# Another order of the maxima and their transposes in the attention of a four-layer backbone

## The reference, cut to what matters

```python
s = einsum('bqhgd,bkhd->bhgqk', q, k) * scale      # latent queries: 512 cached + 1024 latent keys
p = softmax(s, axis=-1)                            # windowed layer: 512 cached + keys within 128, and a sink
o = einsum('bhgqk,bkhd->bqhgd', p, v)              # context queries: 256 context keys
```

## Time and profile before

| what | value |
|---|---|
| three runs, median (lowest to highest) | 3683.17 us (3682.59 to 3685.68) |
| the profiled execution | 3670.98 us, its span 3669.2 us |
| mean granted clock of PE | 0.987 |
| PE busy | 3471.0 us, 95% of the span |
| DVE busy | 2547.2 us, 69% |
| ACT busy | 2166.3 us, 59% |
| POOL busy | 904.4 us, 25% |
| attention of layers 0, 1, 2, 3 | from 399.8, 1337.7, 2207.7, 3026.2 us of the span |

### The profile page before, as it was taken

One profiled execution on the slowest core, in us unless ns is written; L12 is line 12 of the kernel. 1 busy time (PEld: TensorE's weight loads), 2 busy tenths in 40 slices (PEclk: granted clock), 3 DMA queues, 4 the chain that ended last, 5 costly groups with the idle time before them and its releaser, 6 DMA issues. The chain is left out here.

```text
span 3669.2 us, 80042 instructions
## 1 busy us (share of the span) xinstructions
PE 3471.0 (95%) x33644; PEld 2061.8 (56%) x33644; DVE 2547.2 (69%) x3728; ACT 2166.3 (59%) x2859; POOL 904.4 (25%) x739
## 2 busy tenths in 40 slices
PE   6999999999999989999999998888999989999998
PEld 3554566666455555565555565666455545666654
DVE  6426788888457559999755518989553458888864
ACT  5424677877434348888733217777334338888861
POOL 0000144343220014444411001222220003444432
PEclk8999999999999999999999999999999999999999
DMA  6127533332112342333111425443112382222211
GB/s 255 48 85 224 146 80 75 71 83 62 72 36 70 118 127 65 81 78 76 28 72 61 118 95 134 100 97 71 68 43 71 120 225 64 55 55 57 49 54 58
DMA packets 373318, 325.35 MB, mean 89 GB/s; under 512 B 246272, under 2 KB 294080, under 8 KB 371424
## 3 DMA queue, kind: packets, MB, share of 16 engines
q1 hardware_dynamic: 372960, 320.24, 32.1%
HBM read 228.94 MB, written 91.23 MB: 87 GB/s over the span
## 5 line engine op out<-in xcount | busy, mean ns | idle before, releaser
L2242 PE MATMUL bank<-q_slots,k_slots 96*128 96x512 f16 (+7 forms) x3968 | 1050.0, 366 | 26.2 <-PEq L1436 16.2
L798 PE MATMUL bank<-H_hilo,w_hilo 128*128 128x512 f16 (+1 forms) x5760 | 1044.8, 344 | 11.8 <-DVE w_hilo L1048 8.3
L2061 DVE TENSOR_REDUCE max_parts<-bank 128x1 f32<-128x512 f32 (+2 forms) x1536 | 954.0, 644 | 115.4 <-PE bank L2005 110.2
L2318 ACT ACTIVATE p_f<-bank 128x1024 f32<-128x1024 f32 (+2 forms) x768 | 743.0, 967 | 316.6 <-PE bank L2242 300.1
L798 PEld LDWEIGHTS bank<-H_hilo,w_hilo 128*128 128x128 f16 x5760 | 563.4, 98 | 493.0 <-DVE w_hilo L1048 9.3
L2366 DVE TENSOR_TENSOR p_lo<-p_f,p_hi 128x1024 f16<-128x1024 f32 (+2 forms) x576 | 712.7, 1237 | 63.3 <-ACT p_hi L2325 60.1
L2325 ACT ACTIVATE p_hi<-bank 128x1024 f16<-128x1024 f32 (+2 forms) x768 | 740.3, 964 | 0.0
L2005 PE MATMUL bank<-k_slots,q_slots 96*128 96x512 f16 (+4 forms) x1536 | 565.6, 370 | 42.5 <-DVE max_parts L2061 36.5
L2429 POOL TENSOR_TENSOR p_lo<-p_f,p_hi 128x1024 f16<-128x1024 f32 x192 | 414.3, 2158 | 549.8 <-ACT p_hi L2325 549.8
L2242 PEld LDWEIGHTS bank<-q_slots,k_slots 96*128 96x128 f16 (+2 forms) x3968 | 345.7, 98 | 285.2 <-issue 51.3
L1012 ACT ACTIVATE z_ring<-bank 128x512 f32<-128x512 f32 (+1 forms) x192 | 87.5, 528 | 428.6 <-PE bank L798 414.0
(11 more groups left out here) (205 smaller groups left out, 4054.9 us busy)
## 6 DMA issues: line engine op xcount, KB each, us to landing
ada_w<-in_w_ada SPq DMA_DIRECT2D x48, 768.0 KB, 6.3
gate<-z_ring SPq DMA_DIRECT2D x32, 640.0 KB, 3.3
gate_rows<-gate SPq DMA_DIRECT2D x32, 640.0 KB, 3.9
q_slots<-q_mla SPq DMA_DIRECT2D x64, 240.0 KB, 3.2
k_mla<-H_hilo SPq DMA_DIRECT2D x64, 224.0 KB, 3.2
k_slots<-k_mla SPq DMA_DIRECT2D x64, 224.0 KB, 4.6
cq_hilo<-v_scratch SPq DMA_DIRECT2D x64, 224.0 KB, 4.2
v_lo_hi_one<-v_scratch SPq DMA_DIRECT2D x64, 224.0 KB, 4.2
```

The costliest lines, as they stand in the source:

```text
L798: ins = pe.matmul(dst, lhs(a, k), rhs(b, k), start=(k == 0 and n == 0), stop=(k == nk - 1 and n == 2))
L2061: found = dve.tensor_reduce(mx[:, o, t, c:c + 1], mb[:, 0:nk], AX.X, ALU.max)
L2242: scored = pe.matmul(dst, lhs, rhs, start=(m == 0), stop=(m == len(ops) - 1), skip_group_check=swa)
L2318: act.activation(p32[:, g % 3, 0:cols], src, ACT.Exp, scale=scale).then_inc(s_p32.h, 1)
```

## The change

The two lists get another order. In layers 0, 1 and 3 the last maximum of unit 1 goes from second in step 3 to first in step 2, its transpose from first in step 4 to first in step 3. The last maximum of unit 2 goes from first in step 1 to second in step 2, its transpose from step 3 to step 4. Six of unit 1's twelve maxima instead of five are made in the head ahead (three in step 10, one in 11, two in 12). In layer 2 the same is done one step earlier throughout: last maximum of unit 1 first in step 1, its transpose in step 2, that of unit 2 in step 3; five of eight maxima instead of four are made ahead, and the modulation entry goes from step 8 to step 7. The third edit is one more item in a list of places for the entries made ahead of layer 2's first head.

```diff
@@ attention @@
         if swa:
-            own = [b_[4:6] + c_[:1], c_[1:] + b_[6:7], [turn(2)] + b_[7:], [turn(1)], [], [], [], [], []]
-            ahead = [[], [], [], a_[:2], a_[2:4], a_[4:6], a_[6:], b_[:3], [turn(0)] + b_[3:4] + mod]
+            own = [b_[5:7] + c_[:1], b_[7:] + c_[1:], [turn(1)], [turn(2)], [], [], [], [], []]
+            ahead = [[], [], [], a_[:2], a_[2:4], a_[4:6], a_[6:] + b_[:1], b_[1:3] + mod, [turn(0)] + b_[3:5]]
         else:
-            own = [b_[5:7] + c_[:1], c_[1:] + b_[7:9], b_[9:11], [turn(2)] + b_[11:], [turn(1)]] + [[]] * 8
-            ahead = [[]] * 4 + [a_[:2], a_[2:4], a_[4:6], a_[6:8], a_[8:10], a_[10:], b_[:2], mod + b_[2:3],
-                                [turn(0)] + b_[3:5]]
+            own = [b_[6:9], b_[9:11] + c_[:1], b_[11:] + c_[1:], [turn(1)], [turn(2)]] + [[]] * 8
+            ahead = [[]] * 4 + [a_[:2], a_[2:4], a_[4:6], a_[6:8], a_[8:10], a_[10:], b_[:3], mod + b_[3:4],
+                                [turn(0)] + b_[4:6]]
...
-        at_tile = [3, 3, 4, 5, 5, 6, 7, 7, 8, 8, 9, 9, 10, 10, 10, 10] if swa else [3 + k * 2 // 5 for k in range(NE)]
+        at_tile = [3, 3, 4, 5, 5, 6, 7, 7, 8, 8, 9, 9, 10, 10, 10, 10, 10] if swa else [3 + k * 2 // 5 for k in range(NE)]
```

## The result

The changed kernel takes 3712.53 us (median of 4 runs, 3709.76 to 3713.23), the kernel before beside it 3684.43 us (3682.59 to 3686.33): a ratio of 1.0075, 95% interval 1.0057 to 1.0092, or 28 us slower. The prediction was 3698 us, between 3672 and 3716, with 0.67 for slower: sign and range held, the size was half of what came. The profiled execution took 3712.46 us (span 3710.7).

What follows compares the result with a forecast made beforehand. PE bounds layers 0 and 3; PE and DVE are level in layers 1 and 2. Layer 1 +11.5, layers 0 and 3 +15.5, layer 2 -12.1 sum to +15 us on the median 3683.17: 3698 us, range 3672 to 3716.

Steps and rivals of the forecast that it cites:

- Part (a): Unit 1's last maximum goes ahead of the reciprocal in step 2; 1.05 us of DVE work leaves POOL's shadow.
- the chain: From unit 1's reciprocal through POOL's normalisation and p_lo to the end of DVE's p_lo of step 3: 4.08 us, fixed.
- Eight pairs +11.5 us: Layer 1: DVE's work outside the chain grows 1.05 us a head, less absorbed waits; +1.44 us a pair of heads.
- The bound of +17 us: Layer 1's upper bound: 16 heads at 1.05 us each, with nothing absorbed by waits.
- the wait in step 12: Layer 1: DVE's wait of 0.25 us in step 12 of each head absorbs part of its delay.
- Part (b): One 512-column maximum moves from a head's step 0 to steps 10 to 12 of the head before; same work for DVE.
- Layers 0 and 3: DVE's delay reaches PE at a maximum's bank: new waits 0.35 and 0.80 us, +7.8 us a layer, +15.5 in both.
- Layer 2: Windowed layer: schedule gains 5.2 us, regained granted clock 6.9 us; sum -12.1 us, bounds -27.6 to +9.6.
- the waits were PE's own loss: Rival: freeing PE's waits at L2030 makes the kernel faster, -25 us, 3658 us; chance 0.14.
- New low clock: Rival: PE's new 1.8 us wait in step 5 of layer 1 lowers its clock, adding 14 us, 3712 us; chance 0.12.

Runs made afterwards that it cites:

- kernel with the last maximum first: Kernel before, layer 1 alone: five maxima ahead as before, unit 1's last maximum first in step 2, transposes in steps 3 and 4; 3693.12 us.
- the kernel without the second collision: Changed kernel, but in step 5 of layer 1 DVE takes p_lo of step 4 before the step's first maximum; 3692.71 us, ratio 1.0034 to the kernel before.

## Why the prediction was right, and where it fell short

*Part (a), the chain.* Right. The chain kept its 4.08 us, POOL was first by 0.59 us (0.3 to 0.5 was forecast), and p_lo of step 3 ended 1.08 us after POOL's. The kernel with the last maximum first keeps the chain (4.09 us) and loses just what left its shadow, 4.1 us; with the reciprocal first in the changed kernel the loss is gone. GPSIMD Engine Reference of the Trainium skill, section Key points, says that the two engines contend at instructions with two SBUF inputs. The trace agrees that they do, and shows that order decides which of them pays: at the second place they met both before and after the change, and DVE's instruction took 1.21 us when first and 3.10 when second.

*Layer 1, the term that failed.* "Eight pairs +11.5 us" was measured at +39.6. Two things were wrong in it.
- The waits that were to absorb part of the delay did not. The step took off 0.25 us a head for the wait in step 12; after the change the same instruction still has it:

```profile
1578.40 1.38 DVE L2061 TENSOR_REDUCE max_parts<-bank 128x1 f32<-128x512 f32 x2 [0.26 <-PE bank L2005]
```

  Why it stays is argued and not shown: PE is held by DVE in step 5 (1.56 us), so that DVE would find it no earlier in step 12. That makes the term 16 x 1.05 = 16.8, and 17.9 is what the kernel without the second collision shows.
- The second collision, up to 21.7 us, was not looked for. The prediction followed DVE's delayed p_lo to the maxima behind it and to PE's wait; behind three maxima stood another p_lo, which had been 0.68 us ahead of POOL's. A delay of 1.05 us turns that around, and one of 0.26, in the kernel with the last maximum first, does not (0.30 us of the lead were left). The bound of +17 us assumed too that a delay is only handed on.

*Part (b).* Six ahead at no cost: right in layer 1 (1.0 us in one execution).

*Layers 0 and 3.* Right in mechanism and nearly in size: +6.5 and +6.8 for 7.8 each. The new waits stand at the very maximum named. PE in layer 0, an even head and an odd one:

```profile
622.45 0.39 PE L2005 MATMUL bank<-k_slots,q_slots 96*128 96x512 f16 x1 [0.59 <-DVE max_parts L2061]
...
656.70 0.39 PE L2005 MATMUL bank<-k_slots,q_slots 96*128 96x512 f16 x1 [0.39 <-DVE max_parts L2061]
```

0.80 and 0.35 were forecast. L2030 keeps 1.6 and 1.3 us. That the early reciprocal takes the whole loss away, and PE's wait at this maximum with it, says that it came from the same chain.

*Layer 2.* The term had two parts. The schedule is right: 0.65 us a pair was forecast, 0.60 was measured (44.42 less 43.82). For the clock the forecast named the 1.76 us wait, and low time did go with that wait; but 6.9 us was read from an execution with 25.5 us of it. The three profiled kernels with the old lists and a clock of 0.93 have 51 to 52, and against their 375.5 us the term is worth about 26, and not 12.1.

*The sum.* 39.6 + 6.5 + 6.8 - 26.4 (375.5 less 349.1) gives 26.5 us, and the ratio of medians 28. The forecast's +15 was the sum of a layer 1 too small by 28 us and a layer 2 too small by 14. Its total was nearer than its parts, and that the result fell inside the range is in part luck: layer 1 alone, at +39.6, went past its bound of +17, and the clock's gain in layer 2 made up for half of the excess.

*The rivals.* Of "the waits were PE's own loss", the layer 2 share holds, but in layers 0, 1 and 3 the waits at L2030 went down and the time rose. Perfetto Trace Analysis of the Trainium skill, section Optimization Strategies, says that when the matmul engine idles, the engines that block it are to be optimized. The trace shows that moving work off one wait is not that: PE waited 40 us less at the transpose, DVE had no less to do, and the kernel became slower. "New low clock" was nearly nothing: layer 1 kept a mean of 0.99, with waits of 1.56 us in it, so waits of that length do not always bring the low level. Its low time rose from 8.0 to 13.9 us, which at half the speed is 3 us at most (an estimate), and not the rival's 14.

## What to carry to other kernels

Before an operation is moved ahead of another, ask what the second one starts on other engines, and what work was done while that chain ran: the moved work's whole length is paid if nothing takes its place. Follow a delay on through the queue until it has met every instruction that another engine could block, and note by how much each one is ahead, as an order held by less than the delay turns around and costs once more. And read a granted clock from several executions of the kernel before its gain is priced.

## What the runs showed of the hardware

- Of two p_lo (128x1024, two SBUF inputs) on DVE and POOL that meet, the one that starts first is not disturbed, and the other pays. DVE's took 1.21 us when it started 0.68, 0.49 or 0.30 us ahead of POOL's, and POOL's then 2.52, 2.71 and 2.91 instead of 2.13. DVE's took 2.47 us when 0.74 behind, 2.62 when 0.59 behind and 3.10 when 0.10 behind. In each of these six meetings the second one ended 3.20 to 3.21 us after the first one's start.
- DVE's maxima, which read PSUM, took some 0.6 us each beside a p_lo of POOL (four in 2.47 us at 1567.17, POOL's from 1566.72 to 1569.24), as they do alone.
- The order counts at the scale of 0.1 us: with POOL ahead by 0.10 us in the changed kernel, up to 21.7 us of layer 1 hung on it, in 13 heads.
- With the same lists in layer 2, kernels had 23 to 25 us of low clock there in some executions and 51 to 52 in others, and the stage took 361 to 363 or 375 to 376 us accordingly.
